# Moving transposes between the DMA queue and TensorE in a hybrid decoder trunk on eight cores

## The reference, cut to what matters

```python
h = rmsnorm(x, g_mix)
u, q, f, v, og, ga, gb = split(h @ w_in)
ya = (pool_mix(u) @ w_pool * pool_scale) @ w_a       # branch A: trailing means
fg = lb + (1 - lb) * sigmoid(f); k = 1 - fg          # branch B: gated recurrence
S_t = diag(fg_t) S_(t-1) + k_t outer v_t             # 4 heads of 128 x 128
o_t = S_t^T silu(q_t)
yb = (rmsnorm_per_head(o) * g_onorm * silu(og)) @ w_b
x  = x + (sigmoid(ga) * ya + sigmoid(gb) * yb) @ w_out
x  = x + square(relu(rmsnorm(x, g_mlp) @ w_up)) @ w_down
y  = rmsnorm(x, g_final)
```

## Time and profile before

| | |
|---|---|
| median of 3 runs | 906.6 us (905.15 to 932.52) |
| the profiled execution | 905.27 us |
| its span on the slowest core (core 5) | 903.7 us |
| spans of the eight cores | 899.3 to 903.7 us |
| busy on core 5: TensorE, VectorE, ScalarE, GpSimd | 97%, 46%, 40%, 13% |
| DMA | 95.95 MB, mean 106 GB/s |
| groups 0 to 3 of the first pass, by the start of line 1039 | 124.91, 226.51, 328.11 and, in group 3, 428.2 us |

### The profile page before, as it was taken

One profiled execution on the slowest core, in us unless ns is written; L12 is line 12 of the kernel. 1 busy time (PEld: TensorE's weight loads), 2 busy tenths in 40 slices (PEclk: granted clock), 3 DMA queues, 4 the chain that ended last, 5 costly groups with the idle time before them and its releaser, 6 DMA issues.

```text
span 903.7 us, 15014 instructions; the slowest of 8 cores (899.3 to 903.7 us)
## 1 busy us (share of the span) xinstructions
PE 872.7 (97%) x4985; PEld 451.3 (50%) x4985; DVE 417.5 (46%) x693; ACT 361.6 (40%) x639; POOL 120.8 (13%) x190
## 2 busy tenths in 40 slices
PE   4999989999999999999999999999999999999997
PEld 2667544454445444465444444444444444688443
DVE  4665545776477675754543214442143311334122
ACT  3655336665376636641333313332133322233222
POOL 3113310145003421153000000000000000000000
PEclk9999999999999999999999999999999999999999
DMA  9999953338404749986999052200420011100111
GB/s 173 166 169 195 177 137 128 106 96 193 167 1 140 174 129 214 182 120 115 194 216 188 7 141 72 70 1 18 123 94 0 1 47 47 73 2 2 45 51 72
DMA packets 85704, 95.95 MB, mean 106 GB/s; under 512 B 31965, under 2 KB 66397, under 8 KB 85612
## 3 DMA queue, kind: packets, MB, share of 16 engines
q1 hardware_dynamic: 61644, 64.57, 24.8%
q0 software_dynamic: 23984, 30.41, 22.8%
HBM read 92.35 MB, written 26.11 MB: 131 GB/s over the span
## 4 chain that ended last, share of the span: by engine, by line
PE 86%; DMA 4%; DVE 3%; ACT 3%; issue 3%; POOL 0%; SPq 0%; DVEq 0%; ACTq 0%; POOLq 0%
PE ps L591 47%; PE ps L1335 24%; PE ps L603 9%; ACT arena L569 3%; DMA arena<-arena 2%; PE ps L1039 2%; DMA arena<-w_in 1%; DVE arena L672 1%; DVE arena L572 1%; DMA arena<-meta 1%; PE ps L891 0%; PE ps L750 0%; PE ps L767 0%; PE ps L1333 0%; PE ps L762 0%
## 5 line engine op out<-in xcount | busy, mean ns | idle before, releaser
L591 PE MATMUL ps<-arena 128*128 128x512 bf16 (+2 forms) x2720 | 494.7, 339 | 9.1 <-ACT arena L569 6.9
L591 PEld LDWEIGHTS ps<-arena 128*128 128x128 bf16 x2720 | 261.0, 98 | 215.7 <-issue 20.9
L569 ACT ACTIVATE arena<-ps 128x512 f32<-128x512 f32 (+5 forms) x332 | 193.0, 597 | 285.8 <-PE ps L591 211.1
L569 ACT ACTIVATE arena<-arena 128x1024 bf16<-128x1024 f32 (+6 forms) x234 | 152.4, 666 | 249.6 <-DVE arena L1349 170.0
L1335 PE MATMUL ps<-arena 128*128 128x512 bf16 x1024 | 222.0, 379 | 0.0
L572 DVE TENSOR_TENSOR arena<-arena 128x512 bf16<-128x512 f32 (+6 forms) x214 | 147.0, 694 | 133.9 <-ACT arena L569 125.6
L1335 PEld LDWEIGHTS ps<-arena 128*128 128x128 bf16 x1024 | 100.0, 98 | 121.4 <-issue 1.3
L572 DVE TENSOR_TENSOR arena<-ps,arena 128x512 f32<-128x512 f32 (+5 forms) x151 | 103.7, 701 | 80.7 <-PE ps L591 27.5
L603 PE MATMUL ps<-arena 128*128 128x512 bf16 (+2 forms) x480 | 107.5, 379 | 0.7 <-DMA arena<-w_in 0.7
L1349 DVE SCALAR_TENSOR_TENSOR arena<-ps,arena 128x1024 f32<-128x1024 f32 (+2 forms) x18 | 22.0, 1223 | 152.5 <-PE ps L1335 137.9
L572 POOL TENSOR_TENSOR arena<-arena 128x512 f32<-128x512 bf16 (+7 forms) x78 | 76.4, 986 | 75.9 <-DMA arena<-sth 25.3
(11 more groups left out here) (97 smaller groups left out, 242.7 us busy)
## 6 DMA issues: line engine op xcount, KB each, us to landing
arena<-xp SPq DMA_DIRECT2D x32, 512.0 KB, 6.1
arena<-w_in POOLq DMA_DIRECT2D x9, 1024.0 KB, 20.9
x1d<-arena SPq DMA_DIRECT2D x16, 512.0 KB, 5.4
arena<-w_up POOLq DMA_DIRECT2D x8, 1024.0 KB, 10.8
arena<-x1d SPq DMA_DIRECT2D x16, 512.0 KB, 3.8
y_p<-arena SPq DMA_DIRECT2D x15, 512.0 KB, 2.9
arena<-w_down POOLq DMA_DIRECT2D x5, 1024.0 KB, 26.0
h2d<-arena SPq DMA_DIRECT2D x16, 256.0 KB, 5.0
```

The source lines that it names most:

```text
L569: P.add("act", lambda h: h.activation(out=out, in_=in_, func=func, **kw), reads=reads, writes=writes)
L591: i = h.matmul(ps[:, bb, 0:m], lhsT=wfn(k), rhs=rfn(k, c, m), start=(k == 0), stop=(k == K - 1))
```

## The change

1. In group 0, row tiles 0 and 1 of the next group are turned by TensorE instead of by DMA (`g > 0 or t >= 2`), and `scale_rows` covers columns 256 to 512 there.
2. In groups 1 and 2, k is turned by DMA: behind `prep_k` of each head SP issues two transposes of 128x256 elements into two new buffers `ktD`, one for tiles 0 and 1, one for tiles 2 and 3. They lie where `ktT` and the second `t2` buffer lie. The TensorE transposes and ScalarE copies of these groups go; the state update reads `ktD`.
3. In groups 1 and 2, the output rows of tiles 0 to 2 are turned by DMA straight into `obT`; tile 3 stays with TensorE.

```diff
--- before.py
+++ after.py
@@ -413,6 +413,10 @@
         x0 = [view(o_ft + 4096 * i, 1024, F32) for i in range(4)]
         r_xn0 = [region(o_qp + 2048 * i, 2048) for i in range(4)]
         xn0 = [view(o_qp + 2048 * i, 1024, BF16) for i in range(4)]
+
+        o_kd = [o_ktT, o_sg + 4352]
+        r_kd = [region(o, 2048, 4) for o in o_kd]
+        ktD = [view(o, 1024, BF16).rearrange("p (t h n) -> p t h n", t=2, h=4) for o in o_kd]
         r_sga = [region(o_sg + 1088 * i, 1088) for i in range(2)]
         sga = [view(o_sg + 1088 * i, 544, BF16) for i in range(2)]
         r_t2 = [region(o_sg + 2176 + 2112 * i, 2112) for i in range(2)]
@@ -691,6 +695,10 @@
             t1 = T1[h_]
             P.add("dve", lambda h: h.scalar_tensor_tensor(out=kt[:, h_, c:544], in0=t1[:, c:544], scalar=oml[:, h_:h_ + 1], in1=T3[i][:, c - 16:528], op0=ALU.mult, op1=ALU.mult),
                   reads=[r_T1[h_].bufs[0], b_oml] + r_T3[i].bufs, writes=[r_kt.bufs[h_]])
+            if g in (1, 2):
+                for j in range(2):
+                    P.add("sp", lambda h, j=j: h.dma_start_transpose(out=ktD[j][:, :, h_, :], in_=kt[:, h_, 32 + 256 * j:288 + 256 * j]),
+                          reads=[r_kt.bufs[h_]], writes=[r_kd[j].bufs[h_]], dma=True)
 
         def prep_q(h_):
             tt(qt[:, h_, 32:544], q32[:, h_, 32:544], T2[h_][:, 32:544], ALU.mult, [r_q.bufs[h_]] + r_T2[h_].bufs, [r_qt.bufs[h_]])
@@ -735,13 +743,17 @@
             bo = 4 + i
             pO = ps[:, bo, :].rearrange("p (h n) -> p h n", h=4)
 
+            by_dma = g in (1, 2)
+            kT, bkT = (ktD[t // 2][:, t % 2], r_kd[t // 2].bufs) if by_dma else (ktT[i], r_ktT[i].bufs)
+
             def a():
                 def tr(h):
                     for k in range(4):
                         x = h.transpose(out=psT[:, k, :], in_=kt[:, k, c:c + 128], identity=ident_b)
                     return x
-                P.add("pe", tr, reads=r_kt.bufs + [b_idb], writes=[b_pT[0]])
-                act(ktT[i], psT[:, 0:4, :], AF.Copy, [b_pT[0]], r_ktT[i].bufs)
+                if not by_dma:
+                    P.add("pe", tr, reads=r_kt.bufs + [b_idb], writes=[b_pT[0]])
+                    act(ktT[i], psT[:, 0:4, :], AF.Copy, [b_pT[0]], r_ktT[i].bufs)
                 b = banks(1)
                 pA = ps[:, b, :].rearrange("p (h n) -> p h n", h=4)
 
@@ -764,9 +776,9 @@
 
                 def mu(h):
                     for k in range(4):
-                        x = h.matmul(pU[:, k, :], lhsT=ktT[i][:, k, :], rhs=v[:, t, k * 128:(k + 1) * 128], start=True, stop=True)
+                        x = h.matmul(pU[:, k, :], lhsT=kT[:, k, :], rhs=v[:, t, k * 128:(k + 1) * 128], start=True, stop=True)
                     return x
-                P.add("pe", mu, reads=r_ktT[i].bufs + [vb], writes=[b_ps[6]])
+                P.add("pe", mu, reads=bkT + [vb], writes=[b_ps[6]])
                 P.add("pe", mo, reads=r_AT[i].bufs + [vb] + r_qt.bufs + r_Smb.bufs, writes=[b_ps[bo]])
                 tt(T, pU, Sm, ALU.add, [b_ps[6]] + r_Sm.bufs, r_T.bufs)
                 act(osq, ps[:, bo, :], AF.Square, [b_ps[bo]], r_oq.bufs)
@@ -787,6 +799,9 @@
 
             def p():
                 done.append((g, t))
+                if by_dma and t < 3:
+                    P.add("sp", lambda h: h.dma_start_transpose(out=obT[:, :, 128 * t:128 * t + 128], in_=ob[i]), reads=r_obr[i].bufs, writes=[r_ob.bufs[t]], dma=True)
+                    return
                 ob_transposes(ob[i], 128, r_obr[i].bufs)
                 act(obT[:, :, 128 * t:128 * t + 128], psT[:, 4:8, :], AF.Copy, [b_pT[1]], [r_ob.bufs[t]])
             return a, o, n1, state_cast if t < 3 else (lambda: None), n2, p
@@ -868,9 +883,9 @@
                 else:
                     act(wa[:, gg, 0:512], ps[:, b, :], AF.Copy, [b_ps[b]], [raw])
 
-        def scale_rows(X, bufs, w, k, n):
-
-            P.add("dve", lambda h: h.tensor_scalar(out=X[:, k, 0:n], in0=X[:, k, 0:n], scalar1=w[:, k:k + 1], scalar2=None, op0=ALU.mult), reads=bufs + [b_pk], writes=bufs)
+        def scale_rows(X, bufs, w, k, n, c=0):
+
+            P.add("dve", lambda h: h.tensor_scalar(out=X[:, k, c:n], in0=X[:, k, c:n], scalar1=w[:, k:k + 1], scalar2=None, op0=ALU.mult), reads=bufs + [b_pk], writes=bufs)
 
         def fold_wb():
             for c in range(4):
@@ -1100,6 +1115,13 @@
                 U(lambda: u_f(m))
             for r in r_T2 + r_T3 + r_u[0:4 if g == 0 else 2] + r_pt:
                 activate(r)
+            if g in (1, 2):
+                for r in r_kd:
+                    activate(r)
+                A(35, lambda: [activate(r) for r in r_t2])
+            if last:
+                for r in r_ktT:
+                    activate(r)
 
             b0 = tl.t
 
@@ -1149,7 +1171,7 @@
 
                 def pre(t):
                     i = xl[t]
-                    rfin.append(rms1(xr[i], r_x[i].bufs, 128, t, N[:, :, 128 * t:128 * t + 128], bN[t], True))
+                    rfin.append(rms1(xr[i], r_x[i].bufs, 128, t, N[:, :, 128 * t:128 * t + 128], bN[t], g > 0 or t >= 2))
                 for t, z in enumerate((0, 1, 2, 10.5 if g == 0 else 8)):
                     if g > 0 or t == 3:
                         tl.later(z, lambda t=t: xl.update({t: xload(x_rows(g + 1, t), 128)}))
@@ -1158,7 +1180,7 @@
                     tl.later(z + 2.4, lambda t=t: rfin[t][0]())
                     tl.later(z + 3.6, lambda t=t: (activate(r_hT[(g + 1) % 2]) if t == 0 else None, rfin[t][1]()))
                 for k in range(8):
-                    tl.later((25.7 if g == 0 else 24.2) + 0.6 * k, lambda k=k: scale_rows(N, bN[0:4], gmix, k, 512))
+                    tl.later((25.7 if g == 0 else 24.2) + 0.6 * k, lambda k=k: scale_rows(N, bN[2:4] if g == 0 else bN[0:4], gmix, k, 512, 256 if g == 0 else 0))
             for t, z in enumerate((13.5, 19.5, 22) if g == 0 else (11.5, 14.5, 19.5)):
                 tl.later(z, lambda t=t: xi.update({t: xslice(xload(x_rows(g, t), 128))}))
             for m in range(4):
```

## The result

| | before | after |
|---|---|---|
| time, median (lowest to highest), us | 905.93 (905.15 to 932.52) | 900.3 (899.91 to 954.17) |
| span of the longest core, us | 903.7 (core 5) | 898.4 (core 0) |
| spans of all cores, us | 899.3 to 903.7 | 894.7 to 898.4 |

The ratio of after to before is 0.9938, with a 95% interval of 0.9924 to 0.9953: 5.6 us less by the medians, 0.6%, which is under the 2% that the prediction took as its border. The prediction was 900.9 us, 5.65 us less. In some executions of any version part of the cores show a lower granted clock all through and the time is some per cent longer (932.52 and 954.17 us are of that kind), and all ratios here are of the other executions.

The account below looks back on a forecast made before the run. The prediction took TensorE, busy 97% of the longest span, as the bound. Its terms, -3.4 + 0.9 + 0.1 - 1.9 - 1.35 = -5.65 us, took the median of 906.6 us to 900.9 us, with ends of 897.5 to 904.0 us.

Parts of the forecast that it names:

- Bound and stall (-3.4): Group 0: TensorE's wait behind the reuse of xn and the clock dip go, slowest core against slowest, -3.4 us.
- Rival E: Group 0: the stall stays, now at tile 3's Square or at w_out; 904.4 us, chance 0.07.
- 16 transposes and two evictions (+1.0): Group 0: 16 added TensorE transposes cost 0.9 us, two VectorE evictions 0.1 us.
- k (-1.9): Groups 1 and 2: transpose blocks of tiles 1 to 3 go, 0.32 us each, -1.9 us; tile 0's block counted 0.
- The wait taken as 0: First state update of groups 1 and 2: no wait for k by DMA, at worst 3.6 us a group.
- The bound of 0.41 us a block: k by DMA in groups 1 and 2: 16 blocks at 0.41 us each land by 167.0 us, 7.8 us early.
- Rows (-1.35): Groups 1 and 2: six output-row transpose blocks leave TensorE, -1.35 us, new waits taken as 0.
- rival A: Groups 1 and 2: short waits for tile 2's rows or k eat 3.2 us; 904.2 us, chance 0.12.
- my bound of 6.2 us: Before the first yb: tile 2's rows land within 6.2 us of issue, at 209.7 us, 1.8 us early.
- B: Groups 1 and 2: tile 2's rows land after 14 to 18 us, idling TensorE; 924.5 us, chance 0.05.
- C: Groups 1 and 2: k's blocks land serially at 1309 ns each, two waits of 2.1 us; 905.1 us, chance 0.04.
- D: Groups 1 and 2: 0.60 us waits before yb vanish and tile 0's blocks pay too; 899.1 us, chance 0.20.

Follow-up runs that it names:

- e3: Kernel before, with tiles 2 and 3 of group 0 squared and scaled into two more buffers, all four tiles still turned by DMA; 901.7 us, ratio 0.9947.
- e4: Kernel before, with tile 0 alone turned by TensorE in group 0, k and output rows as before; 903.2 us, ratio 0.9965.
- e1: Kernel before, with only tiles 0 and 1 turned by TensorE in group 0, k and output rows as before; 902.4 us, ratio 0.9952.
- e6: Kernel before, with only k turned by DMA in groups 1 and 2; 906.6 us, ratio 0.9980.
- e7: Kernel before, with only output rows of tiles 0 to 2 turned by DMA in groups 1 and 2; 909.2 us, ratio 1.0003.
- e2: Kernel before, with k and three output tiles by DMA in groups 1 and 2, group 0 as before; 905.1 us, ratio 0.9986.
- e5: e3 with k and three output tiles turned by DMA in groups 1 and 2 as well; 901.4 us, ratio 0.9914.
- e10: e5 run again on another chip; 900.6 us, ratio 0.9929 to the kernel before.
- e8: Changed kernel with k turned by DMA in group 3 too, where 1 MB weight loads run; 901.8 us, ratio 0.9933 to the kernel before.
- e12: e5 with all output rows turned by TensorE again; 900.1 us, ratio 0.9927 to the kernel before.
- e11: e5 with tile 2's output rows turned by TensorE again; 899.8 us, ratio 0.9923 to the kernel before.

## Why the prediction was right, and where it was not

**Bound and stall (-3.4): the mechanism right, the size low.** TensorE bounds the kernel, the stall came from a write behind a late read of `xn` (e3), and both tiles were needed for it to go on all cores (e4). The reading by core 4 as the kernel without a stall held to 0.1 us (14.5 in e3). Rival E is out. e3 has nothing but this term: by its profile it is 903.7 - 900.2 = 3.5 us, by its ratio 4.8 (3.7 to 6.0). The profiles are short of the runs because the stall varies from execution to execution and I had taken it from a mild one: the longest span of the kernel before is 903.7 us there, and 903.7 to 906.5 (median 904.6) in 13 executions on e3's chip, whose own are 899.9 to 900.4.

**16 transposes and two evictions (+1.0): too high.** They cost 0.5 us (24.65 against 24.15), since a wait of 0.43 us went with them. Up to line 1054 the longest core gave 2.87 us where 2.4 was forecast, and part 1 alone gave 4.3 us by its ratio (3.3 to 5.5), which leaves out 2.4. Of it 0.3 us is a shorter group 1 that I had not counted (101.33 on most cores of e1 and e3, 101.60 before): the wait at its first scores is 0.21 us there instead of 0.49. Why it shrinks was not tested.

**k (-1.9): mis-sized.** I took 0.32 us a block, with the turn-round to the next matmul. e6 gives 0.2, the low end, 1.3 us in all: TensorE has to turn round there with or without the block. The wait taken as 0 was 0. The bound of 0.41 us a block is not what one transpose does, since each of two blocks took 2.3 to 3.9 us to land; but they overlap, and the 16 blocks were there 14.3 us after the first issue at the latest, at 167.7 us on core 0, before the state update at 171.7.

**Rows (-1.35): mis-sized, and the waits taken as 0 were not always 0.** Alone they shorten groups 1 and 2 by 1.15 us (e7). On top of k it is less: e2 against e6 has group 1 shorter by 0.5 to 0.6 us, group 2 by 0.3 and group 3 longer by 0.4, which leaves 0.5. And on some cores in e2, e5, e7 and e10 the first yb waited up to 2.04 us where 0.60 is the rule, each time for tile 2's rows. It is rival A's wait. The landing was near my bound of 6.2 us (5.4 in e2, at most 7.0 in the others). What I had wrong is the issue: in e2 it came 4.9 us before the yb was due (306.75 to 311.69 us), where I had taken 8.0 from the old transpose (203.48 to 211.51), because a state load that waits for a store stands ahead of it on SP. In the changed kernel's two profiles no core shows the wait, but the thinnest cover there is 0.3 us (rows landed 0.67 us before the yb, of which 0.35 are always needed), and one core of e8, which has the same groups 1 and 2, waits 1.19 us.

Group 3, where nothing was changed but buffers, grew by 0.35 us, to 100.64. It does so in each version with k and all three rows by DMA, and not with k alone (e6, e12), rows alone (e7, 100.35) or rows of two tiles (e11). But it is not one wait. On core 0 of the changed kernel its first matmul of scores (line 762, 750 before) waits for ScalarE:

```profile
367.37 0.22 PE L762 MATMUL ps<-arena 128*64 128x128 bf16 x1 [0.63 <-ACT arena L573]
```

It waited 0.21 us for VectorE on core 5 before. ScalarE is not later there: in both kernels its instruction at that place starts 0.26 us after the first of TensorE's transposes of k (366.36 to 366.62 us; 372.00 to 372.26 before). Only in the changed kernel do the scores wait for its end. In e2, e5 and e10 that wait is 0.28 us, and the rest stands just ahead of the output projection (core 1 of e2):

```profile
422.87 1.45 PE L1054 MATMUL ps<-arena 128*128 128x512 bf16 x6 [0.40 <-DVE arena L576]
```

Why the matmuls come to want these results was not found.

**The sum.** Groups 1 to 3 gave 2.4 us (1.55 + 1.21 - 0.35), and without the 0.3 that part 1 gives in group 1, 2.1 us, where 3.25 was forecast. As whole kernels, part 1 gave 4.3 us where 2.4 was forecast, and k and rows 1.3 us (0.4 to 2.2) where 3.25 was. The two misses, +1.9 and -1.95, cancel. That the total is right to 0.1 us, 5.6 against 5.65, is luck; what was right is the mechanism of part 1 and the direction of k. The stated range also does not follow from its ends: they add up to 898.7 to 905.0 us, not 897.5 to 904.0.

**The rivals.** B did not come in groups 1 and 2: landings of at most 6.6 us, under the 8 from which it was to decide. e8 shows it in single executions when the loads of weights run beside it. C is out: one after another at 1.31 us, the 16 blocks of k would take 21 us. They were issued within 10.4 us and each landed at most 3.9 us after its issue, so all were there 14.3 us after the first at the latest. The page "VectorE: DVE Perf Modes" of the Trainium skill, which gives the DMA crossbar 1309 ns for 128x128 (The three transpose paths), is not borne out as a price per block in a row. D did not come: the 0.60 us wait before yb stayed, and tile 0's block paid nothing. A came in part, on single cores of other versions; its account of where the time goes, rows of tile 2 before yb, is what e2, e7 and e10 show.

## What to carry to other kernels

A transfer's lateness costs nothing until something wants its source or its target: before an operation is moved to another engine, look which buffer the waiting instruction wants, since here two more buffers did the same as moving 16 transposes to TensorE. A small DMA transpose can be a good trade for TensorE time where it is issued long before it is wanted and no large loads run (k), and gained nothing where the cover was thin (rows). When an engine hands work to an in-order queue, look at what stands ahead of it there and what that waits for, not only at the moved work's own landing. When the profile names who ended a wait, check by the times: here it named VectorE in waits that a landing ended. And take a matmul block at its bare time, without the turn-round, when it goes.

## What the runs showed of the hardware

- A DMA transpose held SP for 1.19 us (median) with 2 blocks of 128x128, 1.20 with 4 and 1.4 to 1.6 with 8 (line 657 in e4 and in the changed kernel), single ones for up to 3.2. So the time hardly grows with the size, and by the block many small ones cost SP more than one large one.
- Two blocks landed in 2.3 us (median) in quiet stretches and in up to 13.0 beside 1 MB weight loads (e8).
- TensorE went on 0.35 us (in four places 0.38 or 0.44) after the landing of the DMA that it waited for, in 21 waits of e2, e5, e7, e8 and e10.
- The window of 5 us in which a wait of 4.07 us on TensorE ended had a granted clock of 0.76, the next 0.90 (e8, core 0); within it, from 378 to 380 us, it was 0.50, about the lower of the two levels (1.2 GHz). The wait of 4.27 us was followed by 0.52 in a window of 2 us; in the changed kernel, without either, that window had 1.00.
- How group 0 turns its tiles shifts waits in later groups by tenths: group 2 is 100.22 us in the changed kernel and 100.43 in e2 and e10, which differ from it only there. That the PSUM banks then come in another order is only argued.
